# Expert stage with two 32-row half blocks per pass, each with its own expert's weights, from five weight buffers fed through one indirect queue

## The chip, the cores and the metric

The kernel runs on one core of one Trainium2 chip. The metric is the device time of one execution in microseconds (us); the median of three executions is given. A profile of one execution goes with it.

## The reference, cut to what matters

One step of a hybrid decoder for 512 prompt tokens and 64 sample tokens together (N = 576, D = 1024), all in 32-bit floats. After token mixing (convolution branch, sparse attention, output projection, layer norm) comes the channel stage, which the change is about:

```python
def hier_moe(x, w_rg, b_rg, w_re, b_re, w_eg, w_eu, w_ed):
    N = x.shape[0]
    gl = (x @ w_rg).astype(jnp.float32) + b_rg.astype(jnp.float32)
    pg = jax.nn.softmax(gl, axis=-1)
    grp = jnp.argmax(gl, axis=-1)
    ...
    top_p, top_i = lax.top_k(jax.nn.softmax(el_g, axis=-1), TOP_K_IN_GROUP)
    ...
    eid = grp[:, None] * EXPERTS_PER_GROUP + top_i
    ...
    hidden = jax.nn.silu(hg) * hu * combine[..., None].astype(x.dtype)
    return jnp.einsum('nef,efd->nd', hidden, w_ed)
x  = LN2(alpha * x1 + HierMoE(x1) + sigmoid(x1 @ w_pg) * (p[i] @ w_pp))
```

Every token goes to 2 of 32 experts, both of its one group of 8; so there are 1152 token-expert pairs. An expert's weights are a gate and an up matrix (1024 x 256 each) and a down matrix (256 x 1024): 3.146 MB. Run on its inputs, the reference's router gives experts 0 to 31 these numbers of pairs: 179 126 147 14 71 91 65 143 | 6 2 17 2 14 10 9 16 | 16 49 4 12 33 22 29 25 | 5 14 5 0 15 2 7 2.

## The kernel before, in words

All phases up to the layer norm LN1 (projection, convolution, index search, attention, w_o) stay as they are. The phases that matter here, in the order of TensorE's job list: the gate and embedding products `pg` and `pp` (L1145, L1152, L1393; weights on SyncE's queue through three buffers), among them `rank` (L1401: counts of pairs per expert and each pair's rank in its expert), and `slot_lists` (L1245: for each block the rows to gather); then the expert stage; then the sum of each token's two rows (L1573, L1581) with LN2.

Expert stage before. `blocks_and_slots` (L2293 on) turns the counts into blocks of 64 rows. Each of the 32 experts has one base block, whether it is full or not; 17 over blocks (NOVER) take what lies above 64 pairs of an expert. The 49 blocks run in a fixed order, base, base, over. A block is one pass: 64 rows of x1 are gathered into 128 partitions (row halves above each other, L1088, six buffers), transposed (L1507), multiplied with gate and up (L1525: 16 products, each a 128x64 stationary tile and 256 columns, gate in PSUM partitions 0 to 63, up in 64 to 127; every 32-bit product is two instructions), turned into `hid` by ScalarE and VectorE (L1889, L2363, L2367), transposed (L1535), multiplied with down (L1549: 4 products, 512 columns), copied to `ys` (L1895) and scattered (L1095).

Weights before. SyncE loads the base experts' weights with plain transfers into three buffers (L874 gate and up, L875 down); `up_in` and `down_in` are waited for apart. It issues the first three early (at 892 us of the span), and load e when the down product of base block e-3 is done (`y_full`). GpSimd loads the over blocks' weights with indirect transfers (L1073 into two buffers, L1080 into one); where a buffer already holds the expert, or the block is empty, the index is out of bounds and nothing moves, but the transfer is issued and signals its end.

TensorE works one pass ahead. The order of its instructions is written out, and it is the same before and after the change:

```python
            for p in range(NBLK):
                up_half(p, 0)
                if p:
                    hid_turn(p - 1)
                up_half(p, 1)
                if p + 1 < NBLK:
                    turn(p + 1)
                if p:
                    down(p - 1)
```

So `down(p)` comes after `up_half(p+1, 1)` and directly ahead of `up_half(p+2, 0)`. Each engine's instructions, GpSimd's transfers with their waits among them, run in program order.

## Time and profile before

| | |
|---|---|
| median of 3 executions | 1356.88 us (1349.61 to 1359.10) |
| profiled execution, span | 1355.7 us |
| TensorE matmul busy | 1207.4 us (89%) |
| VectorE / ScalarE / GpSimd busy | 765.2 / 411.4 / 573.1 us |
| first up product to last down product of the expert stage | 983.1 to 1315.8 us |
| moved by all transfers | 281.46 MB |

How to read it: the span of the profiled execution is 1.2 us under the median. Busy shares are averages over phases with different limits; the expert stage is a quarter of the span and has to be read by itself. SyncE and GpSimd issue transfers on two queues (q1 and q0 in the profile), which share the core's 16 DMA engines. PEclk 1.00 is TensorE at 2.4 GHz, 0.50 at 1.2 GHz.

### The profile page before, as it was taken

The numbers are of one execution on the slowest core, as the hardware profiler recorded it, in microseconds if no ns is written. First come the engines' busy times: TensorE is split into PE (matmuls) and PEld (weight loads), VectorE is DVE, ScalarE is ACT, GpSimd is POOL, SyncE is SP. The second block draws the span as 40 slices with busy tenths as digits, with TensorE's granted clock in tenths as the row PEclk, the third lists the DMA queues.
The fourth block names the chain that finished last, engine by engine and source line by source line (L and its number), as shares of the span: only waits on it lengthen the run. The fifth ranks groups of instructions, "written<-read, shape, count | busy, mean of one in ns | idle before, by whom it ended". The sixth has DMA issues, their size and how long they took to land.

```text
span 1355.7 us, 18796 instructions
## 1 busy us (share of the span) xinstructions
PE 1207.4 (89%) x7242; PEld 744.3 (55%) x7242; DVE 765.2 (56%) x1414; ACT 411.4 (30%) x852; POOL 573.1 (42%) x518
## 2 busy tenths in 40 slices
PE   4699999989499886878999899998998989998996
PEld 3425677777355543335565458887754544554542
DVE  1629999999987988696745134432622212222216
ACT  3450134364265467664121221231111111111110
POOL 5000067878776666657776000000233443443420
PEclk9799999989798987878999999999999999999998
DMA  9501222223266565658897630363199998999945
GB/s 326 192 27 36 93 63 63 63 82 116 72 199 179 156 198 169 203 178 249 298 300 235 208 98 31 95 271 132 43 394 421 389 416 345 368 416 419 400 156 205
DMA packets 92839, 281.46 MB, mean 208 GB/s; under 512 B 17959, under 2 KB 50551, under 8 KB 81799
## 3 DMA queue, kind: packets, MB, share of 16 engines
q1 hardware_dynamic: 54672, 165.64, 32.6%
q0 software_dynamic: 35520, 111.22, 24.7%
q10 hardware_dynamic: 2559, 3.40, 0.8%
q8 instruction: 58, 0.95, 0.3%
q14 instruction: 30, 0.25, 0.1%
HBM read 300.94 MB, written 23.11 MB: 239 GB/s over the span
## 4 chain that ended last, share of the span: by engine, by line
PE 49%; DVE 27%; DMA 10%; POOL 6%; issue 4%; ACT 3%; SPq 1%; POOLq 0%; DVEq 0%; ACTq 0%
PE ps L1525 10%; PE ps L1549 6%; POOL arena L1045 6%; DVE arena L1962 6%; DVE arena L1961 5%; DVE arena L1963 5%; PE ps L1139 5%; PE ps L1145 5%; PE ps L1369 4%; DMA arena<-scr_x,arena 3%; PE ps L1361 3%; DMA arena<-in_w_in 2%; DMA arena<-in_w_dn,arena 2%; PE ps L1507 2%; PE ps L1227 2%
## 5 line engine op out<-in xcount | busy, mean ns | idle before, releaser
L1045 POOL DMA_INDIRECT arena<-in_cache_kv,arena x256 | 267.7, 1046 | 125.2 <-issue 74.0
L1139 PE MATMUL ps<-arena 128*128 128x288 f32 (+2 forms) x1120 | 297.6, 427 | 1.1 <-ACT arena L1693 1.1
L1139 PEld LDWEIGHTS ps<-arena 128*128 128x128 f32 (+1 forms) x1120 | 211.0, 191 | 85.5 <-issue 30.0
L1525 PE MATMUL ps<-arena 128*64 128x256 f32 x1568 | 189.5, 384 | 5.6 <-DMA arena<-in_w_gu 3.5
L1525 PEld LDWEIGHTS ps<-arena 128*64 128x64 f32 x1568 | 109.2, 138 | 83.6 <-issue 28.0
L1095 POOL DMA_INDIRECT scr_ypair<-arena x49 | 50.5, 1030 | 184.5 <-ACT arena L1895 165.2
L1088 POOL DMA_INDIRECT arena<-scr_x,arena x49 | 50.0, 1021 | 172.1 <-DVE arena L2343 157.5
L1616 ACT ACTIVATE arena<-ps 128x256 f32<-128x256 f32 (+5 forms) x138 | 57.9, 429 | 203.9 <-PE ps L1361 64.4
L1024 POOL TENSOR_TENSOR arena<-arena 128x816 f32<-128x816 f32 x58 | 103.0, 1776 | 17.8 <-ACT arena L1634 11.2
L1145 PE MATMUL ps<-arena 128*128 128x256 f32 (+4 forms) x544 | 105.6, 357 | 0.9 <-ACT arena L1838 0.6
L1549 PE MATMUL ps<-arena 128*64 128x512 f32 x392 | 98.4, 624 | 8.0 <-DMA arena<-in_w_dn,arena 7.9
L1145 PEld LDWEIGHTS ps<-arena 128*128 128x128 f32 (+1 forms) x544 | 92.5, 194 | 14.0 <-issue 2.2
L2359 DVE COPY arena<-ps 128x512 f32<-128x512 f32 x49 | 33.9, 692 | 109.4 <-PE ps L1507 109.3
L2374 DVE COPY arena<-ps 128x128 f32<-128x128 f32 x49 | 14.3, 292 | 142.4 <-PE ps L1535 142.4
L1961 DVE MAX8 arena<-arena 128x8 f32<-128x2052 f32 x32 | 73.6, 2299 | 1.1
L1962 DVE FIND_INDEX8 arena<-arena 128x8 uint32<-128x2052 f32 x32 | 73.3, 2290 | 0.0
L1963 DVE MATCH_REPLACE8 arena<-arena 128x2052 f32<-128x2052 f32 x32 | 73.0, 2280 | 0.0
L1361 PE MATMUL ps<-arena 128*128 128x288 f32 (+1 forms) x192 | 68.1, 508 | 2.8 <-DVE arena L2148 2.2
L1895 ACT ACTIVATE arena<-ps 128x512 f32<-128x512 f32 x49 | 29.3, 597 | 122.5 <-PE ps L1549 122.5
L1634 ACT ACTIVATE arena<-arena 128x816 f32<-128x816 f32 x60 | 57.0, 970 | 28.6 <-POOL arena L1024 26.3
L1889 ACT ACTIVATE arena<-ps 128x128 f32<-128x128 f32 x49 | 13.6, 278 | 169.8 <-PE ps L1525 169.8
L2053 DVE SCALAR_TENSOR_TENSOR arena<-arena 128x512 f32<-128x512 f32 x120 | 56.9, 515 | 2.0
(350 smaller groups left out, 1687.1 us busy)
## 6 DMA issues: line engine op xcount, KB each, us to landing
arena<-in_w_gu SPq DMA_DIRECT2D x32, 2048.0 KB, 12.3
arena<-in_w_dn SPq DMA_DIRECT2D x32, 1024.0 KB, 15.6
arena<-in_w_in SPq DMA_DIRECT2D x20, 1024.0 KB, 5.6
arena<-scr_q SPq DMA_DIRECT2D x32, 256.0 KB, 4.6
arena<-in_cache_kv,arena POOLq DMA_INDIRECT x256, 3.9
arena<-in_w_o SPq DMA_DIRECT2D x4, 1024.0 KB, 5.4
arena<-in_w_pg SPq DMA_DIRECT2D x4, 1024.0 KB, 9.0
arena<-scr_ypair SPq DMA_DIRECT2D x4, 1024.0 KB, 8.0
```

The costliest lines, as they stand in the source:

```text
L1024: nc.gpsimd.tensor_tensor(a[:, 0:CLEN], a[:, 0:CLEN], p[:, 0:CLEN], ALU.add).then_inc(conv_add, 1)
L1045: pl.indirect_dma_start(unit_rows[:, 2 * j + t, half * H * HD:(half + 1) * H * HD], None, I["cache_kv"].rearrange("n (h d) -> (n h) d", h= ...
L1139: mm = nc.tensor.matmul(out, w[:, k], hT[:, k, a:b], start=(k == 0), stop=(k == KC - 1))
L1145: mm = nc.tensor.matmul(out, hT[:, k, at:at + rows], w[:, k], start=(k == 0), stop=(k == KC - 1))
L1361: mm = nc.tensor.matmul(ps[:, 0:n], w[:, c], src[:, c, at:at + n], start=(c == 0), stop=(c == CC - 1))
L1525: mm = nc.tensor.matmul(PS[2 + p % 2][64 * half:64 * half + 64, 0:2 * P], xT[:, p % 3, j, 64 * h:64 * h + 64], w[:, k, half, :], start=(k ...
L1549: mm = nc.tensor.matmul(PS[5 + p % 2][64 * half:64 * half + 64, :], hidT[:, p % 2, c * 64:c * 64 + 64], w[:, c, half * 512:(half + 1) * 51 ...
L1616: return nc.scalar.activation(handed(job, width, rows), PS[NUM[job] % RING][0:rows, 0:width], func, scale=scale)
L1634: nc.scalar.activation(prod[:, k % 3, 0:CLEN], glu[:, c, w:w + CLEN], cp, scale=tap).then_inc(prod_ready, 1)
L1961: step(V.max(m, work))
L1962: V.max_index(idxu[:, r * 8:r * 8 + 8], m, work)
L1963: step(V.match_replace(work, m, work, TAKEN))
```

## The change

Blocks have 32 rows (BLK) and no division into base and over: expert e has ceil(count/32) half blocks, and all half blocks are sorted by expert. A pass takes two half blocks, called visits 2p and 2p+1, each with its own expert's weights: `up_half` and `down` issue twice as many products, each with a 128x32 stationary tile, for four strips of 32 PSUM partitions (gate and up, times two visits). There are NBLK = 34 passes and NVISIT = 68 visits, which holds any routing.

Visit q uses weight buffer q % 5. `visit_blocks` cuts the sorted list into five runs (14, 14, 14, 13, 13 half blocks) and gives run j to buffer j, so neighbours in a run often share an expert. A visit whose buffer already holds its expert, or that is empty, gets an index out of bounds: its transfer is issued and moves nothing. Gate, up and down lie together in one array `w_ex` (24 KB a row); one indirect transfer of 3.146 MB, issued by GpSimd, fills a buffer and signals `expert_in[q % 5]`. SyncE loads no expert weights any more. The first three loads are issued once the table is ready, loads 3 and 4 after the last `pp` job, load q from 5 on when `y_full` says that pass (q-5)//2 has done its down product. `up_half(p, 0)` waits for the loads of visits 2p and 2p+1. The gather buffers are five, three of them filled first.

```diff
-BLK = 64
-NOVER = (2 * N - NE) // (BLK + 1)
-NBLK = NE + NOVER
-XR = 6
+BLK = 32
+NSLOT = 5
+NBLK = -(-(2 * N + NE * (BLK - 1)) // BLK // 2)
+NVISIT = 2 * NBLK
+XR = 5
+XEARLY = 3
 YR = 4
...
+def visit_blocks():
+
+    lengths = [len(range(j, NVISIT, NSLOT)) for j in range(NSLOT)]
+    return [sum(lengths[:q % NSLOT]) + q // NSLOT for q in range(NVISIT)]
+
+
+VISITS = visit_blocks()
...
-        ra = region(x_at, ki_at)
         rb = region(q_at + 2 * D, b_end)
         rk_ = region(ki_at + NT * D, q_at)
-        eset = [ra(3 * KC * F), rb(3 * KC * F), rb(3 * KC * F)]
+        ESIZE = 3 * KC * F
         w_at = x_at - WSLOTS * KC * GW
-        over_up = [view(ht_at + i * 2 * KC * F, (KC, 2, F)) for i in range(2)]
-        over_down = view(ht_at + 4 * KC * F, (FC, D))
-        assert ht_at + KC * N == w_at and 5 * KC * F <= KC * N + WSLOTS * KC * GW
+        assert ht_at + KC * N == w_at and ht_at + 2 * ESIZE >= x_at
+        eset = [rb(ESIZE), rb(ESIZE)] + [view(ht_at + i * ESIZE, (ESIZE,)) for i in (2, 0, 1)]
+        xg_at = ht_at + 3 * ESIZE
+        assert xg_at + XR * 512 <= ki_at
...
-                    for e in range(3):
-                        load_expert(e)
...
-            for e in range(3, NE):
-                sp.wait_ge(y_full, POS[("base", e - 3)] + 1)
-                load_expert(e)
...
+            def load_expert(q):
+                if q >= NSLOT:
+                    pl.wait_ge(y_full, (q - NSLOT) // 2 + 1)
+                pl.indirect_dma_start(eset[q % NSLOT], None, I["w_ex"],
+                                      bass.IndirectOffsetOnAxis(ap=widx[:, q:q + 1], axis=0),
+                                      bounds_check=NE * P - 1, oob_is_err=False).then_inc(expert_in[q % NSLOT], 16)
 
             def gather(p):
...
+            pl.wait_ge(wr_in, 48)
+            pl.wait_ge(full, after("pT", NT - 1))
+            nc.gpsimd.memset(xg[:, 0:XEARLY], 0.0).then_inc(xg_clear, 1)
+            pl.wait_ge(xg_clear, 1)
+            pl.wait_ge(table_ready, 1)
+            for q in range(3):
+                load_expert(q)
             pl.wait_ge(glist_ready, 1)
             pl.wait_ge(x1_out, 16 * NT)
-            for p in range(XR):
+            for p in range(XEARLY):
                 gather(p)
-            load_over_up(0)
-            load_over_down(0)
-            load_over_up(1)
+            pl.wait_ge(full, after("pp", 3, NT - 1))
+            for q in range(3, NSLOT):
+                load_expert(q)
+            pl.wait_ge(taken, TAKEN_AT[("pp", 3, NT - 1)])
+            nc.gpsimd.memset(xg[:, XEARLY:], 0.0).then_inc(xg_clear, 1)
+            pl.wait_ge(xg_clear, 2)
+            for p in range(XEARLY, XR):
+                gather(p)
             for p in range(NBLK):
                 if p and p + XR - 1 < NBLK:
                     gather(p + XR - 1)
+                for q in range(2 * p + NSLOT, 2 * p + NSLOT + 2):
+                    if q < NVISIT:
+                        load_expert(q)
                 scatter(p)
...
-                for half in range(2):
-                    for n in range(2 * NT):
-                        rows = TILES[n % NT][1]
-                        mm = nc.tensor.matmul(PS[4][64 * half:64 * half + 64, 0:NBLK], in_place[0:rows, n, :], in_block[0:rows, n, :],
-                                              start=(n == 0), stop=(n == 2 * NT - 1))
+                for n in range(2 * NT):
+                    rows = TILES[n % NT][1]
+                    for strip in range(4):
+                        mm = nc.tensor.matmul(PS[4][BLK * strip:BLK * strip + BLK, 0:NBLK], in_place[0:rows, n, :],
+                                              in_block[0:rows, n, strip % 2::2], start=(n == 0), stop=(n == 2 * NT - 1))
                 mm.then_inc(plist_full, 1)
...
             def up_half(p, part):
-                kind, n = BLOCKS[p]
-                k = n if kind == "base" else OVERS.index(n)
-                w = up_weights(eset[n % 3]) if kind == "base" else over_up[k % 2]
                 if part == 0:
-                    if kind == "base":
-                        pe.wait_ge(up_in[n % 3], 16 * (n // 3 + 1))
-                    else:
-                        pe.wait_ge(over_up_in[k % 2], 16 * (k // 2 + 1))
                     pe.wait_ge(xt_drained, p + 1)
                     if p >= 2:
                         pe.wait_ge(hid_ready, p - 1)
+                    for q in (2 * p, 2 * p + 1):
+                        pe.wait_ge(expert_in[q % NSLOT], 16 * (q // NSLOT + 1))
+                w = [up_weights(eset[q % NSLOT]) for q in (2 * p, 2 * p + 1)]
                 for k in range(4 * part, 4 * part + 4):
                     h, j = divmod(k, 4)
                     for half in range(2):
-                        mm = nc.tensor.matmul(PS[2 + p % 2][64 * half:64 * half + 64, 0:2 * P],
-                                              xT[:, p % 3, j, 64 * h:64 * h + 64], w[:, k, half, :],
-                                              start=(k == 0), stop=(k == KC - 1))
+                        for sub in range(2):
+                            r = 64 * half + BLK * sub
+                            mm = nc.tensor.matmul(PS[2 + p % 2][r:r + BLK, 0:2 * P],
+                                                  xT[:, p % 3, j, 64 * h + BLK * sub:64 * h + BLK * sub + BLK], w[sub][:, k, half, :],
+                                                  start=(k == 0), stop=(k == KC - 1))
...
             def down(p):
-                kind, n = BLOCKS[p]
-                w = down_weights(eset[n % 3]) if kind == "base" else over_down
-                if kind == "base":
-                    pe.wait_ge(down_in[n % 3], 16 * (n // 3 + 1))
-                else:
-                    pe.wait_ge(over_down_in, 16 * (OVERS.index(n) + 1))
+                w = [down_weights(eset[q % NSLOT]) for q in (2 * p, 2 * p + 1)]
                 pe.wait_ge(ht_drained, p + 1)
                 if p >= 2:
                     pe.wait_ge(y_act, p - 1)
                 for c in range(FC):
                     for half in range(2):
-                        mm = nc.tensor.matmul(PS[5 + p % 2][64 * half:64 * half + 64, :], hidT[:, p % 2, c * 64:c * 64 + 64],
-                                              w[:, c, half * 512:(half + 1) * 512], start=(c == 0), stop=(c == FC - 1))
+                        for sub in range(2):
+                            r = 64 * half + BLK * sub
+                            mm = nc.tensor.matmul(PS[5 + p % 2][r:r + BLK, :], hidT[:, p % 2, c * 64 + BLK * sub:c * 64 + BLK * sub + BLK],
+                                                  w[sub][:, c, half * 512:(half + 1) * 512], start=(c == 0), stop=(c == FC - 1))
                 mm.then_inc(y_full, 1)
...
-                nb, incl, base, t1 = [blocks[:, i, :] for i in range(4)]
-                step(V.tensor_scalar(nb, cnt, float(BLK), None, ALU.is_gt))
-                for k in range(2, -(-N // BLK)):
-                    step(V.tensor_scalar(t1, cnt, float(k * BLK), None, ALU.is_gt))
-                    step(V.tensor_tensor(nb, nb, t1, ALU.add))
+                nb, incl, base, whole = [blocks[:, i, :] for i in range(4)]
+                whole = whole.bitcast(I32)
+                step(V.tensor_scalar(whole, cnt, float(BLK - 1), None, ALU.add))
+                step(V.tensor_scalar(whole, whole, 5, None, ALU.logical_shift_right))
+                step(V.tensor_copy(nb, whole))
                 step(V.tensor_tensor_scan(incl, C["ones"][:, 0:NE], nb, 0.0, ALU.mult, ALU.add))
-                step(V.tensor_tensor(base, incl, nb, ALU.subtract))
-                V.tensor_tensor(cmp_, C["iota"][:, 0:NOVER].unsqueeze(2).to_broadcast([P, NOVER, NE]),
-                                incl.unsqueeze(1).to_broadcast([P, NOVER, NE]), ALU.is_ge)
-                step(V.scalar_tensor_tensor(base, base, float(BLK), C["overslot"], ALU.mult, ALU.add))
-                V.memset(turns[:, 0:2], -1.0)
-                step(V.tensor_reduce(table, cmp_, AX.X, ALU.add))
-                V.tensor_copy(turns[:, 2::2], table[:, 0:EARLY])
-                step(V.tensor_copy(turns[:, 3::2], table[:, EARLY:]))
-                now, last, other = turns[:, 2:], turns[:, 1:1 + NOVER], turns[:, 0:NOVER]
-                V.tensor_tensor(again[:, 0], now, other, ALU.is_equal)
-                V.tensor_tensor(again[:, 1], now, last, ALU.is_equal)
-                step(V.tensor_scalar(again[:, 2], last, float(NE), None, ALU.is_ge))
-                step(V.tensor_tensor(again[:, 2], again[:, 2], again[:, 0], ALU.mult))
-                step(V.tensor_tensor(again[:, 1], again[:, 1], again[:, 2], ALU.add))
-                for i in range(2):
-                    step(V.scalar_tensor_tensor(again[:, i], again[:, i], float(NE), now, ALU.mult, ALU.add))
-                V.tensor_scalar(widx, again[:, 0:2], float(P), C["part"], ALU.mult, ALU.add).then_inc(table_ready, 1)
+                V.memset(turns[:, 0:NSLOT], -1.0)
+                V.tensor_tensor(base, incl, nb, ALU.subtract)
+                step(V.tensor_tensor(cmp_, C["visit"].unsqueeze(2).to_broadcast([P, NVISIT, NE]),
+                                     incl.unsqueeze(1).to_broadcast([P, NVISIT, NE]), ALU.is_ge))
+                now, last = turns[:, NSLOT:], turns[:, 0:NVISIT]
+                step(V.tensor_reduce(now, cmp_, AX.X, ALU.add))
+                step(V.tensor_tensor(again, now, last, ALU.is_equal))
+                step(V.scalar_tensor_tensor(again, again, float(NE), now, ALU.mult, ALU.add))
+                V.tensor_scalar(widx, again, float(P), C["part"], ALU.mult, ALU.add).then_inc(table_ready, 1)
                 rk = ranks[:, 0:NT * NE].rearrange("p (t e) -> p t e", t=NT)
-                step(V.tensor_scalar(over, rk, float(BLK), None, ALU.is_ge))
-                V.tensor_tensor(rk, rk, C["baseslot"].unsqueeze(1).to_broadcast([P, NT, NE]), ALU.add)
-                step(V.tensor_tensor(over, over, base.unsqueeze(1).to_broadcast([P, NT, NE]), ALU.mult))
```

## Rows read from the trace of the kernel before

**Rows 1.** Windows: length, busy us by engine, PEclk, DMA share, GB/s.
```profile
983.00:1315.80 332.80, 315.26 (x2201) 160.92 (x2201) 73.61 (x205) 42.29 (x97) 126.50 (x125) 0.98 0.94 378
1000.00:1020.00 20.00, 20.00 (x143) 10.19 (x141) 4.80 (x14) 2.63 (x6) 8.18 (x8) 1.00 1.00 417
```
**Rows 2.** Timeline of TensorE, 1038 to 1062 us: start, length, what.
```profile
1040.90 1.95 PE L1525 MATMUL ps<-arena 128*64 128x256 f32 x16
1042.78 0.66 PE L1507 MATMUL ps<-arena 128*128 128x128 f32 x4
1047.39 3.68 PE L1549 MATMUL ps<-arena 128*64 128x512 f32 x8 [3.96 <-DMA arena<-in_w_dn,arena]
1050.86 2.67 PE L1525 MATMUL ps<-arena 128*64 128x256 f32 x16
...
1053.72 1.95 PE L1525 MATMUL ps<-arena 128*64 128x256 f32 x16
1055.60 0.66 PE L1507 MATMUL ps<-arena 128*128 128x128 f32 x4
1056.19 1.94 PE L1549 MATMUL ps<-arena 128*64 128x512 f32 x8
1057.95 1.90 PE L1525 MATMUL ps<-arena 128*64 128x256 f32 x16
...
1060.04 1.95 PE L1525 MATMUL ps<-arena 128*64 128x256 f32 x16
```
**Rows 3.** Groups by line and shape: engine, op, shapes, count, busy us, mean ns.
```profile
L1525 PE MATMUL ps<-arena 128*64 128x256 f32 x1568 | 189.5, 384 | 5.6 <-DMA arena<-in_w_gu 3.5 <-DVE arena L2359 1.9 <-DMA arena<-in_w_gu,arena 0.2
L1549 PE MATMUL ps<-arena 128*64 128x512 f32 x392 | 98.4, 624 | 8.0 <-DMA arena<-in_w_dn,arena 7.9
L1209 PE MATMUL ps<-arena 128*8 128x320 f32 x256 | 18.7, 432 | 0.0
```
**Rows 4.** Queues in the expert stage, 983.1 to 1315.8 us: packets, MB, share.
```profile
q1 hardware_dynamic: 8352, 91.23, 66.1%
q0 software_dynamic: 12176, 34.27, 27.0%
```
**Rows 5.** Timeline: ScalarE's copy, then GpSimd's transfers around 996 and 1297 us.
```profile
994.78 0.60 ACT L1895 ACTIVATE arena<-ps 128x512 f32<-128x512 f32 x1 [2.18 <-PE ps L1549]
996.21 1.03 POOL L1095 DMA_INDIRECT scr_ypair<-arena  x1 [10.55 <-ACT arena L1895]
...
1295.38 1.04 POOL L1080 DMA_INDIRECT arena<-in_w_dn,arena  x1 [0.30 <-issue]
1296.72 1.01 POOL L1073 DMA_INDIRECT arena<-in_w_gu,arena  x1 [0.30 <-issue]
```
**Rows 6.** Transfers issued at 1295.38, 1296.72, 1308.03, 1095.12 us: us to landing.
```profile
arena<-in_w_dn,arena POOLq DMA_INDIRECT x1, 2.1
arena<-in_w_gu,arena POOLq DMA_INDIRECT x1, 8.7
arena<-in_w_dn,arena POOLq DMA_INDIRECT x1, 5.8
arena<-scr_x,arena POOLq DMA_INDIRECT x1, 23.8
```
**Rows 7.** Chain of waits ahead of the expert stage: start, length, what.
```profile
913.57 8.72 DMA arena<-in_w_pp
...
922.33 6.41 PE ps L1393 x20
```
**Rows 8.** Timeline: SyncE's first expert load; the table's last steps; first gather.
```profile
892.36 0.58 SPq L874 DMA_DIRECT2D arena<-in_w_gu  x1
...
952.25 0.72 DVE L2299 TENSOR_TENSOR arena<-arena 128x544 f32<-128x544 f32 x1
...
955.39 0.24 DVE L2314 TENSOR_SCALAR arena<-arena 128x34 int32<-128x34 f32 x1
...
973.73 1.20 POOL L1088 DMA_INDIRECT arena<-scr_x,arena  x1 [157.52 <-DVE arena L2343]
...
983.06 3.67 PE L1525 MATMUL ps<-arena 128*64 128x256 f32 x32 [1.07 <-DVE arena L2359]
```

96 lines of the change are left out of this document (21 added, 75 removed).

## The prediction, made before the changed kernel was run

> **What bounds the kernel now.** I read the table of windows first, for the stretch that the change touches: between 983.0 and 1315.8 us TensorE is busy 315 of 332.8 us [rows 1]. So the expert stage is TensorE's, with the transfers close behind: in an undisturbed stretch they move 417 GB/s at a DMA share of 1.00, over the stage 378 GB/s [rows 1]. TensorE's timeline gives the pitch: the second half of the up product starts at 1053.72 and the next pass's at 1060.04, 6.32 us a pass [rows 2]. 49 passes are 310 us, and some 23 us are waits and what they leave behind. One such wait is in the same rows: TensorE stands 3.96 us, then the down product takes 3.68 us instead of 1.94 and the first half of the next up product 2.67 instead of 1.90. A wait of about 4 us costs another 2.5 us, because TensorE goes on at 1.2 GHz for some 5 us. Last the queues: q1 moves 91.2 MB (29 of the 32 base experts), q0 34.3 MB [rows 4].
>
> **How many loads the change makes.** This is counted from the routing. ceil(count/32) summed over the experts is 55 half blocks (30 of experts 0 to 7). The five runs take positions 0-13, 14-27, 28-41, 42-54 and 55-67 of the sorted list. So buffer 0 sees experts 0, 1, 2 (3 loads), buffer 1 sees 2 to 7 (6), buffer 2 sees 7 to 18 (12), buffer 3 sees 19 to 31 without 27 (12), and buffer 4 only empty visits. That is 33 loads, 104 MB, against 32 base experts and about 25 MB of over blocks before: counted in the same way, 8 gate/up loads and 9 down loads are 26.2 MB, and the row traffic of 1152 pairs is 9.4 MB, together 35.7 MB, where the row of q0 has 34.3 (a few gathers lie ahead of it) [rows 4]. The counting is sound.
>
> **Part 1, fewer passes.** 34 instead of 49. Is a pass as long as before? Up is 64 instructions instead of 32, each on a quarter of the array's columns. Today a 64-column instruction costs 189.5/1568 = 121 ns, 32 of them 3.87 us; down is 8 x 251 ns = 2.0 us. The nearest row with four strips is L1209: 18.7/256 = 73 ns for 320 columns, so 58 ns for 256 and 117 for 512: up 3.7 us, down 16 x 117 = 1.9 us [rows 3]. The strips overlap four deep, and I keep 6.32 us a pass. Bounds: 5.9 (an even better overlap, hardly any weight-load cost) and 6.9 (10% lost). By itself this takes 15 x 6.32 = 95 us off.
>
> **Part 2, when a load may start.** This decides. Load 2p+5 reuses the buffer of visit 2p and is issued when `down(p)` is done. TensorE's next instruction after `down(p)` is `up_half(p+2, 0)`, and that waits for visits 2p+4 and 2p+5. So the second visit of every pass gets its weights with no lead at all; the first visit's (2p+6, for pass p+3) have one pass. Before, load e had the over and base passes between base e-3 and e, three or four, for its lead. Now price it:
> - From `y_full` to GpSimd's transfer: ScalarE's copy ends at 995.38, the scatter waiting for it starts at 996.21, 0.83 us; two transfers in a row are 1.33 us apart [rows 5].
> - A transfer that moves nothing lands 2.1 us after its start on an idle queue, one of 1.05 MB after 5.8 us, one of 2.1 MB after 8.7 us [rows 6]. One step further, 3.15 MB after 11.6 us (with the 417 GB/s of [rows 1] from the 5.8 on: 10.8, the lower bound).
> - q0 is served in order: a gather of a few hundred KB issued behind weights took 23.8 us [rows 6]. So an empty transfer behind a full one is late too.
>
> So every pass from pass 2 on waits at least 0.83 + 2.1 = 2.9 us, even where nothing has to move; and where its second visit has a new expert, 0.83 + 11.6 = 12.4 us, plus 2.5 us at the low clock [rows 2].
>
> I went through the 34 passes with these numbers (transfers on q0 one after the other at 7.5 us for 3.146 MB, 1 us for a scatter and a gather between them):
> - 13 passes have a new expert in the second visit (5, 8, 11, 13, 16, 18, 20, 21, 23, 26, 28, 31, 33): 13 x 12.5 = 162.5 us, and 1.5 us where the queue was still at work. It is about every second visit of buffers 2 and 3.
> - 3 passes (3, 15, 25) have an empty second load behind a full first one: it lands 2.1 + 11.6 - 9.2 + 1 = 5.5 us late, 16.5 us.
> - 16 passes wait 2.9 us: 46.4 us. Pass 1 waits 3.3 us for load 3.
> - Low clock after the 16 long waits: 16 x 2.5 = 40 us.
>
> Together 270 us of waits. The other half of what the change brings, 23 MB less, is worth nothing: 33 x 7.5 = 248 us of transfers lie inside a stage of 486 us.
>
> The Trainium skill (DMA: Bandwidth & Descriptors, Anatomy of one DMA) fits a GpSimd transfer as 2.0 us + bytes/436 GB/s, 9.2 us for this load; by that the 13 long waits would be 31 us less and the time 1476. The rows are above it: 8.7 us for 2.1 MB, where the fit gives 6.8. The same page's Rules for kernel authors say to issue early and wait late; this change does the opposite for half its visits, and no other rule there weighs against that.
>
> **Part 3, ahead of the stage.** SyncE issues no expert loads at 892 us [rows 8]. These 9.4 MB lay ahead of the first `pp` slice, for which the chain waits 8.7 us from its issue, 913.57 to 922.28 [rows 7]; TensorE's share of that wait is about 4 us, and some low clock follows. I give 5 us back (bounds 0 and 6). All up to the end of `pp` moves 5 us earlier. Loads 0 to 2 are issued once the table is ready, today after L2314 at 955.6 [rows 8], then 950.6: some 3.5 us until bytes move (5.8 us less the 2.5 us that 1.05 MB take is 3.3 [rows 6]) and 3 x 7.5 us, so q0 is busy until 976.8. The first gather lies behind them and lands near 979 (today issued at 973.73). Transpose and copy follow, and the first up product starts at 980.5 instead of 983.06 [rows 8], a gain of 2.6 us. Bounds: 5 gained, 5 lost, if the gathers come later still. In the table, 14 small VectorE steps go, and compare and sum grow from 544 (0.72 us each [rows 8]) to 2176 elements, some 4 us more in place of 3 us: nothing. `slot_lists` has twice the instructions at half the width: nothing, `pp` follows it on TensorE. The tail stays.
>
> **The sum.** First up product 980.5; first pass 4.7 (no down product yet); 32 x 6.32 = 202.2; waits 162.5 + 1.5 + 16.5 + 46.4 + 3.3 = 230.2; low clock 15 x 2.5 = 37.5: pass 33 starts at 1455.3. Its up product at the low clock, down(32), the chain through `hid` and the last down product take 11.1 us: 1466.4. Today that point is 1315.8 [rows 1]. So +150.6 us on a span of 1355.7 us, 1506.3; the median is 1.2 us above the span, so **1507 us**. For this case alone: 10.8 us landing, 1.5 us of low clock and 5.9 us passes give 1455; 6.9 us passes and 3.5 us of low clock 1540.
>
> **The rivals.**
> - *The loads keep the queue full and TensorE only follows it* (faster). A stage of 33 x 7.5 us and 4 us at the ends, 252 us instead of 333, 5 us gained ahead: 1271 us. For it: today's DMA share is 1.00 in stretches of this stage [rows 1], and the bytes fall by a fifth. Against: only loads 2p+5 and 2p+6 can be outstanding, and buffers 0, 1 and 4, three of five, rarely bring one. It decides at the point where the 34 x 9.2 = 313 us that even empty transfers cost and some 10 us at the ends leave room: 338 us - 323 us, that is one long wait of 15 us. With two or more second visits that load, the change is slower. I count 13.
> - *The short waits let the clock drop as well.* A wait of 2.9 us lies under the one of 3.96 us that did it [rows 2]; if it is enough, 17 more passes pay 2.5 us, 42 us: 1549.
> - *The four strips don't overlap with 32-column tiles at this load.* Then up is 64 x 121 ns and down 16 x 251 ns, 5.9 us more a pass, not hidden by the waits, since the loads start after it: 1507 + 34 x 5.9 = 1707. Against: the 73 ns of L1209 [rows 3].
> - *The change doesn't do what it says:* if the sorted runs saved no load, all 55 visits would load and some 27 passes wait 15 us: 1650 and more. The routing counts speak against it.
>
> **How the numbers follow.** Forecast 0.74 (1455 to 1540), clock drop 0.13, faster 0.04, strips 0.03, no loads saved 0.02, and 0.04 for something that eats most of the loss but leaves it within 1% or a little slower. The range that leaves out no more than 2 in 10 is 1450 to 1555. About 1% is what a measurement of this kernel can tell from no change: faster 0.04, within 1% 0.03, slower 0.93.
>
> **What would show it.** In the changed profile: waits of `up_half` (L1525's successor) on `in_w_ex` of two sizes, 12 to 13 us 13 times and about 3 us 16 times, 230 us in all; a PEclk below 1.00 after each long one; up 3.7 to 3.9 us undisturbed; GpSimd's load issued 0.8 us after the down product's end; DMA moving about 104 MB of weights at a mean near 235 GB/s over the stage; the stage's first up product near 980 us and its last down product near 1466. It would be wrong if a full load landed in well under 10 us, if an empty transfer signalled without the 2 us, or if GpSimd issued load 2p+5 before `down(p)`.

## The result, and the profile after

The changed kernel takes 1518.61 us (median of 4 runs, 1514.29 to 1525.99), the kernel before 1355.74 us beside it (4 runs, 1349.61 to 1359.10). The ratio is 1.1207, interval 1.116 to 1.1254: slower, by 163 us. The profiled run of the changed kernel has a span of 1512.5 us, 6.1 us under its median.

The page of the changed kernel, groups by line (engine, op, shapes, count, then busy us, mean ns, then idle time ahead of them and what ended it):

```profile
L1483 PE MATMUL ps<-arena 128*32 128x256 f32 x2176 | 179.7, 487 | 222.4 <-DMA arena<-in_w_ex,arena 221.4
L1504 PE MATMUL ps<-arena 128*32 128x512 f32 x544 | 65.4, 598 | 0.4 <-DVE arena L2318 0.4
L1033 POOL DMA_INDIRECT arena<-in_w_ex,arena x68 | 67.9, 998 | 478.4 <-PE ps L1504 307.5
```

L1483 is the up product (before: L1525, [rows 3]), L1504 the down product, L1033 the load of a visit's weights. TensorE stands 221.4 us for weights in front of up products. The third row shows the other side of it: GpSimd stands 307.5 us ahead of these loads until a down product is done. The window of the stage, from the first up product to the end of the last down product (length, busy us by engine, PEclk, DMA share, GB/s), answers the first row of [rows 1]:

```profile
980.15:1472.80 492.65, 270.77 (x2886) 117.38 (x2886) 51.60 (x145) 29.12 (x67) 130.77 (x129) 0.78 0.54 210
```

The stage is 492.7 us instead of 332.8. TensorE works less (271 us instead of 315), and so do the 16 DMA engines (share 0.54 instead of 0.94): neither is the bound, they take turns. Queue q0 moves all of it now (queue, packets, MB, share; compare [rows 4]):

```profile
q0 software_dynamic: 14400, 103.05, 53.5%
```

The turns can be seen in the timelines of TensorE and of GpSimd, changed kernel, 1032 to 1069 us (start, length, what, idle time before it in brackets):

```profile
1032.52 1.92 PE L1504 MATMUL ps<-arena 128*32 128x512 f32 x16
1045.95 3.64 PE L1483 MATMUL ps<-arena 128*32 128x256 f32 x32 [11.50 <-DMA arena<-in_w_ex,arena]
1049.52 0.48 PE L1493 MATMUL ps<-arena 128*128 128x128 f32 x1
1049.92 1.94 PE L1483 MATMUL ps<-arena 128*32 128x256 f32 x32
1051.79 0.66 PE L1467 MATMUL ps<-arena 128*128 128x128 f32 x4
1052.38 1.92 PE L1504 MATMUL ps<-arena 128*32 128x512 f32 x16
1057.38 3.31 PE L1483 MATMUL ps<-arena 128*32 128x256 f32 x32 [3.08 <-DMA arena<-in_w_ex,arena]
...
1068.34 1.93 PE L1483 MATMUL ps<-arena 128*32 128x256 f32 x32 [3.08 <-DMA arena<-in_w_ex,arena]
```

```profile
1035.28 0.99 POOL L1033 DMA_INDIRECT arena<-in_w_ex,arena  x1 [6.07 <-PE ps L1504]
...
1055.15 1.00 POOL L1033 DMA_INDIRECT arena<-in_w_ex,arena  x1 [14.90 <-PE ps L1504]
```

A down product ends at 1034.4, GpSimd starts the load that waited for it at 1035.28, and TensorE's very next instruction can start only when it has landed, at 1045.95. The load at 1055.15 is an empty one and costs 3.08 us in the same place. The first half of the up product takes 3.64 us after the long wait, 3.31 after the short one behind it, and 1.93 us, full clock, after the next short one.

### The profile page after: what moved, and what is told of

It is laid out like the page before. It is cut to its first block, busy times and chain, and to the rows that moved or that the text cites. A ratio compares the mean times of both kernels' runs of the same rounds, so it can differ in the third digit from the quotient of the medians.

```text
span 1512.5 us, 19973 instructions
## 1 busy us (share of the span) xinstructions
PE 1155.9 (76%) x7967; PEld 696.2 (46%) x7967; DVE 741.5 (49%) x1331; ACT 398.1 (26%) x822; POOL 575.1 (38%) x523
## 4 chain that ended last, share of the span: by engine, by line
PE 45%; DVE 23%; DMA 18%; POOL 5%; issue 5%; ACT 3%; SPq 1%; POOLq 0%; DVEq 0%; ACTq 0%
DMA arena<-in_w_ex,arena 13%; PE ps L1483 11%; POOL arena L1013 5%; PE ps L1099 5%; DVE arena L1917 5%; DVE arena L1916 5%; DVE arena L1918 5%; PE ps L1504 4%; PE ps L1105 4%; PE ps L1329 4%; PE ps L1321 3%; DMA arena<-in_cache_kv,arena 2%; PE ps L1187 2%; PE ps L1467 1%; DMA arena<-in_w_pp 1%
## 5 line engine op out<-in xcount | busy, mean ns | idle before, releaser
L1483 PE MATMUL ps<-arena 128*32 128x256 f32 x2176 | 179.7, 487 | 222.4 <-DMA arena<-in_w_ex,arena 221.4
L1033 POOL DMA_INDIRECT arena<-in_w_ex,arena x68 | 67.9, 998 | 478.4 <-PE ps L1504 307.5
L1483 PEld LDWEIGHTS ps<-arena 128*32 128x32 f32 x2176 | 83.8, 136 | 312.6 <-issue 289.9
L2318 DVE COPY arena<-ps 128x128 f32<-128x128 f32 x34 | 9.9, 291 | 360.8 <-PE ps L1493 360.8
L1844 ACT ACTIVATE arena<-ps 128x128 f32<-128x128 f32 x34 | 9.4, 277 | 392.7 <-PE ps L1483 392.7
L992 POOL TENSOR_TENSOR arena<-arena 128x816 f32<-128x816 f32 x58 | 102.9, 1775 | 16.9 <-ACT arena L1589 10.2
L1504 PE MATMUL ps<-arena 128*32 128x512 f32 x544 | 65.4, 598 | 0.4 <-DVE arena L2318 0.4
L2303 DVE COPY arena<-ps 128x512 f32<-128x512 f32 x34 | 23.5, 691 | 75.2 <-PE ps L1467 75.1
L1329 PE MATMUL ps<-arena 128*128 128x256 f32 x256 | 55.9, 380 | 0.8 <-DVE arena L2072 0.8
L1139 PE MATMUL ps<-arena 128*128 128x128 f32 x256 | 40.1, 306 | 19.1 <-DMA arena<-in_cache_kv,arena 11.7
```

The costliest lines, as they stand in the source:

```text
L992: nc.gpsimd.tensor_tensor(a[:, 0:CLEN], a[:, 0:CLEN], p[:, 0:CLEN], ALU.add).then_inc(conv_add, 1)
L1033: pl.indirect_dma_start(eset[q % NSLOT], None, I["w_ex"], bass.IndirectOffsetOnAxis(ap=widx[:, q:q + 1], axis=0), bounds_check=NE * P - 1, ...
L1329: mm = nc.tensor.matmul(ps[0:rows, 0:GW], mixT[:, k, at:at + rows], w[:, k], start=(k == 0), stop=(k == KC - 1))
L1483: mm = nc.tensor.matmul(PS[2 + p % 2][r:r + BLK, 0:2 * P], xT[:, p % 3, j, 64 * h + BLK * sub:64 * h + BLK * sub + BLK], w[sub][:, k, half ...
L1504: mm = nc.tensor.matmul(PS[5 + p % 2][r:r + BLK, :], hidT[:, p % 2, c * 64 + BLK * sub:c * 64 + BLK * sub + BLK], w[sub][:, c, half * 512: ...
```

## The experiments

The chips of the first three groups of runs were slower than the one of the last group: the kernel before took 1480.66, 1481.90 and 1480.41 us there, 1351.46 in the last. For the changed kernel, which has a profile on either kind, the difference lies ahead of the expert stage: its first up product comes at 1115.5 us of the span there and at 980.2 on the chip of the result, and its stage is 487.2 us there and 492.7 here. What stands out in the profiles from the slower chips is idle time of TensorE that ends with nothing the profile shows (`<- issue`): 74 to 94 us of it ahead of the stage, in 78 to 92 places, in each of the eleven; none in the two profiles that the result compares, and none ahead of the stage in experiment 10, the last group. The largest group of it in the changed kernel's second profile:

```profile
PE ps L1162 <- issue: 35.4, 44, 4.3
```

L1162 is a product of the attention, far ahead of the expert stage. Experiment 4 comes back to this.

So what is compared is the ratio to the kernel before of the same group, and the length of the stage (first up product to last down product). The changed kernel once more, beside the second group:

> The changed kernel itself, unaltered, beside the others. The first four kernels ran on a chip on which the kernel before took 1481 us instead of 1356, so their times can't be set against the changed kernel's 1519 directly, only their expert stages can (492.7 us in the changed kernel, 332.8 in the one before). Theory: the expert stage is made of the same waits on any chip, 485 to 500 us; 155 to 165 us more than the kernel before, whatever the phases ahead take. Rival: the stage depends on the chip as the phases ahead do, then it is off by more than 10 us.

Measured: 1649.48 us, ratio 1.1165 (1.1104 to 1.1227), stage 487.2 us. TensorE's waits:

```profile
PE ps L1483 <- DMA arena<-in_w_ex,arena: 218.5, 33, 13.2
```

(us in total, times, longest). The loss is the same on both kinds of chip; 1649.48 and 487.2 are what the next runs are held against.

**1. The down product one half product earlier** (ScalarE's copies are swapped in the same way).

```diff
                     hid_turn(p - 1)
-                up_half(p, 1)
                 if p + 1 < NBLK:
                     turn(p + 1)
                 if p:
                     down(p - 1)
+                up_half(p, 1)
```

> The changed kernel with TensorE's order altered so that down(p-1) runs before the second half of up(p): hid_turn(p-1), turn(p+1), down(p-1), up_half(p,1). The same loads, bytes and instructions; only y_full comes 1.9 us earlier relative to the next up product. Theory (a load has no lead over its use): each of the 32 waits of pass 2 on loses 1.9 us, long ones 11.7 to 9.8, short ones 3.1 to 1.2, 62 us, and the half clock after the short ones goes, some 15 us: about 1440 against 1519. Rival (the weights move slower on GpSimd's one queue, or the queue is the bound): the bytes are the same, 1519 stays. Rival (products on 32 columns are slow): 1519 stays as well.

Measured: 1596.36 us, ratio 1.0794 (1.0727 to 1.0862), stage 443.6 us, 43.6 less than the changed kernel's. The waits of this kernel:

```profile
PE ps L1483 <- DMA arena<-in_w_ex,arena: 174.7, 33, 12.0
PE ps L1504 <- DVE arena L2318: 22.3, 17, 1.5
```

Nothing is loaded faster or less often here; each load only starts half an up product (1.9 us) earlier before its use. The short waits fall from 3.08 to 1.35 us, most long ones from 11.5 to between 9.7 and 10.3, and the sum falls by 44 us. A new wait takes 22 us back, that for the copy of `hidT`, which has less time now; as much comes from the clock, since behind a wait of 1.35 us the first half of the up product takes 1.93 us in every row, where it took 3.2 to 3.6 behind most waits of 3.08. So the lead of a load sets its wait, nearly one to one. The stage was expected to lose 77 us and loses 44; the new wait, which the expectation did not have, is the largest part of the difference.

**2. No empty transfers.** The 33 visits that load are written in for this routing, and the other 35 issue nothing and are not waited for.

```diff
+FULL = [0, 1, 2, 3, 6, 8, 11, 12, 17, 18, 22, 23, 26, 27, 28, 30, 32, 33, 37, 38, 41, 42, 43, 47, 48, 50, 52, 53, 56, 57, 58, 63, 67]
...
             def load_expert(q):
+                if q not in FULL:
+                    return
```

> The changed kernel without its 35 transfers that move nothing: the list of the 33 visits that really load is written into the program (counted from the routing of these inputs), the others issue nothing and nobody waits for them. Theory: the 16 waits of 3.1 us go and the half clock after most of them (1.3 to 1.5 us in about 12 passes); the 13 long ones stay at 11.7: 50 + 17 = about 67 us less, 1450. Rival (an empty transfer costs nothing by itself, TensorE would have waited for something else there, such as the gathered rows or the queue's real loads): 1519 to 1500.

Measured: 1590.80 us, ratio 1.0744 (1.0691 to 1.0798), stage 435.0 us. TensorE's waits:

```profile
PE ps L1488 <- DMA arena<-in_w_ex,arena: 180.7, 18, 15.4
```

The short waits are gone, 15 of 33, and the stage is 52 us shorter: 38 us of waits and the clock behind them. The long ones stay, 11.4 to 11.7 us apiece and up to 15.4 where two loads follow each other closely. The empty transfers are about a third of the loss (1.1165 to 1.0744).

**3. Four buffers instead of five.**

```diff
-NSLOT = 5
+NSLOT = 4
```

> The changed kernel with four weight buffers instead of five (runs of 17 half blocks, 32 loads instead of 33). Now both visits of pass p+2 reuse the buffers of pass p and are issued when down(p) is done, so no load has a lead. Theory: waits of 4.3 us where nothing moves (two transfers issued 1.33 us apart), 11.9 to 13.2 where one loads, about 19.4 where both do: some 360 us of waits instead of 218, about 1670. Rival (the total of bytes or the pace of the queue sets the stage): 32 loads instead of 33, 1510.

Measured (one run): 1805.67 us, stage 650.7 us:

```profile
PE ps L1483 <- DMA arena<-in_w_ex,arena: 362.3, 33, 19.2
```

With four buffers neither visit of a pass has a lead. The waits rise from 218.5 to 362.3 us in 33 places as before, and the kernel loses another 156 us.

**4. Gate/up and down loaded apart, each when its own product is done.** The up part of buffer q is released by the up product (`u_full`), nearly a pass earlier than by the down product; down weights are waited for ahead of `down`. In GpSimd's order each gather and each scatter moves behind the gate/up loads of one more pass.

```diff
+            def load_up(q):
+                if q >= NSLOT:
+                    pl.wait_ge(u_full, (q - NSLOT) // 2 + 1)
+                pl.indirect_dma_start(eset[q % NSLOT][:, 0:2 * KC * F], None, I["w_gu"],
...
+            def load_down(q):
                 if q >= NSLOT:
                     pl.wait_ge(y_full, (q - NSLOT) // 2 + 1)
+                pl.indirect_dma_start(eset[q % NSLOT][:, 2 * KC * F:], None, I["w_dn"],
```

> The changed kernel with each load in two transfers: gate and up (2.1 MB) into a buffer as soon as pass p has done its up product (u_full), down (1.05 MB) when it has done its down product (y_full); up waits for the first, down for the second. 136 instead of 68 weight transfers on the same GpSimd queue, the same 104 MB, the same products. Theory: gate and up now have a lead of 8 us and empty ones are never late; waits fall from 218 to some 50 us, but GpSimd issues six transfers of 1.33 us a pass, 8 us, more than TensorE's 6.3: a stage of 280 to 310 us, 1320 to 1350, below both kernels. Rival (GpSimd's queue is the bound of the changed kernel): twice the transfers, no faster than 1519. Rival (32-column products are slow): 1519 less nothing.

Measured: 1478.64 us, ratio 0.9996 (0.9969 to 1.0023), stage 328.5 us. In the second group:

> The kernel with gate/up loaded at u_full and down at y_full once more, beside the changed kernel. On the first chip its stage was 328.5 us, where 280 to 310 was forecast, with gaps of 0.4 to 0.8 us inside runs of products that no engine and no transfer released. Theory (those gaps belong to that chip): where they are absent the stage is 34 x 8.0 to 8.3 us, set by GpSimd's six transfers a pass, 275 to 300 us, and the time 3 to 5% below the kernel before. Rival (the gaps belong to this kernel): again about 328 us and equal to the kernel before.

Measured: 1480.75 us, ratio 0.9983 (0.9957 to 1.0009), stage 329.6 us. The waits of the first of the two in the stage:

```profile
PE ps L1497 <- issue: 27.9, 43, 0.8
PE ps L1497 <- DMA arena<-in_w_gu,arena: 7.8, 4, 2.8
```

All of the loss is gone with the lead given back: 218.5 us of waits for weights become 7.8. But the stage was expected at 280 to 310 us and is 328.5. Timeline of TensorE, `e4_split_again`, 1248 to 1257 us:

```profile
1248.63 1.48 PE L1497 MATMUL ps<-arena 128*32 128x256 f32 x18
1250.81 0.64 PE L1497 MATMUL ps<-arena 128*32 128x256 f32 x5 [0.69 <-issue]
1252.26 0.63 PE L1497 MATMUL ps<-arena 128*32 128x256 f32 x4 [0.82 <-issue]
1253.70 0.64 PE L1497 MATMUL ps<-arena 128*32 128x256 f32 x5 [0.80 <-issue]
1254.27 0.66 PE L1481 MATMUL ps<-arena 128*128 128x128 f32 x4
1254.86 1.92 PE L1520 MATMUL ps<-arena 128*32 128x512 f32 x16
1256.60 1.91 PE L1497 MATMUL ps<-arena 128*32 128x256 f32 x32
```

TensorE stands 0.7 to 0.8 us in the middle of a product, where the program has no wait: the half product that starts at 1248.63 takes 5.7 us, the one at 1256.60 takes 1.9. Over all products of the stage such idle time is 42.5 us in the first of the two profiles and 44.2 in the second. A stage of 328.5 us less 42.5 would be 286, inside what was expected; that is a subtraction and not a run. In the stage of the changed kernel there are no such rows, on either kind of chip: of the 222.4 us of idle time ahead of its up products 221.4 end with a load. But they are the same kind of idle time as the `<- issue` ahead of the stage, which only the profiles from the slower chips have, and both runs of this experiment were made on those. GpSimd's six transfers do not fill a pass either; it stands 2.5 us for an up product in each of these passes:

```profile
1245.07 1.00 POOL L1034 DMA_INDIRECT arena<-in_w_gu,arena  x1 [2.47 <-PE ps L1497]
...
1255.14 1.00 POOL L1034 DMA_INDIRECT arena<-in_w_gu,arena  x1 [2.49 <-PE ps L1497]
```

Experiments 7 and 8 ask what in this kernel brings the gaps out.

**5. The same, with load 2 behind the first gathers.**

```diff
-            for q in range(3):
+            for q in range(2):
                 load_up(q)
                 load_down(q)
...
                 gather(p)
+            for q in range(2, 3):
+                load_up(q)
+                load_down(q)
```

> As e4_split, but of the three loads that are issued once the table is ready only two go out then; the third is issued behind the first three gathers. Theory (expert weights ahead of it hold up the last 256 KB slice of the embedding product's weights, which took 17.9 us in the changed kernel and 2.9 without company): TensorE's wait for that slice falls from 7.9 us in e4_split to under 3, the first up product comes 5 to 8 us earlier, the time is 4 to 8 us less than e4_split. Rival (that slice waits for its own buffer): the wait stays at 8 us, the time is the same.

Measured: 1478.03 us, ratio 0.9973 (0.9946 to 0.9999); 2.7 us under `e4_split_again`, and the two intervals overlap: that the kernel is faster is not shown. In the profiles the wait for the last `pp` slice is 2.5 us instead of 7.7, and the first up product comes at 1103.8 instead of 1112.8; 9.0 us lie between the two in front, of which the wait is 5.2, and the stage is 3.3 us longer (332.8).

**6. Full loads by SyncE with plain transfers, no empty ones.** As experiment 2, the loads from visit 5 on by the other queue, with the experts written in.

```diff
+            for q, e in zip(FULL, EXPERT):
+                if q >= NSLOT:
+                    sp.wait_ge(y_full, (q - NSLOT) // 2 + 1)
+                    sp.dma_start(eset[q % NSLOT], I["w_ex"][e * P:(e + 1) * P, :]).then_inc(plain_in[q % NSLOT], 16)
```

> As e2_no_empty (33 loads, no empty transfers; the visits and experts written into the program from the routing of these inputs), but from visit 5 on the loads are plain transfers issued by SyncE, at the same points (y_full of the pass that last used the buffer). Theory (no lead, whichever queue): a long wait falls only by the 0.8 us of GpSimd's wake-up and the shorter start of a plain transfer, from 11.7 to 9.5 to 10.5 us; stage 435 - 13 x 1.7 = about 413 us. Rival (the single software queue makes the loads slow): waits of 6 us or less, stage below 370 us.

Measured (one run): 1576.05 us, stage 416.2 us:

```profile
PE ps L1497 <- DMA arena<-in_w_ex: 159.1, 17, 13.7
```

A wait is still 10.2 to 10.6 us in most places (11.4 to 11.7 with GpSimd's indirect transfers). The indirect queue costs about 1 us of a wait; the rest is 3.146 MB that start when they are needed.

**7. Half as many products, split loads.** Products with 64 columns as before the change. Gate takes the first visit's weights for all 64 rows and up the second's, so this kernel leaves out half of the mathematics; loads, waits and copies are those of 4.

```diff
-                        for sub in range(2):
-                            r = 64 * half + BLK * sub
-                            mm = nc.tensor.matmul(PS[2 + p % 2][r:r + BLK, 0:2 * P],
...
+                        mm = nc.tensor.matmul(PS[2 + p % 2][64 * half:64 * half + 64, 0:2 * P],
+                                              xT[:, p % 3, j, 64 * h:64 * h + 64], w[half][:, k, half, :],
...
```

> As e4_split (each load in two transfers, issued early), but with 64-column products instead of pairs of 32-column ones: 40 instead of 80 product instructions a pass. All loads, waits and copies stay, but every row is multiplied with only one of its pass's two sets of weights, so the mathematics of half the rows is left out. In e4_split TensorE stood 0.8 us again and again in the second half of the up product, four or five products at a time, with nothing that released it. Theory (TensorE's instructions come too slowly when it no longer waits for weights; their number doubled with the strips): the gaps go, a pass takes the 8.0 us of GpSimd's six transfers, stage 275 to 290 us instead of 329, time 40 to 50 us below e4_split. Rival (GpSimd or the transfers set e4_split's stage and the gaps fill idle time): 320 to 330 us as before.

Measured: 1458.68 us, ratio 0.9844 (0.9827 to 0.986), stage 310.9 us:

```profile
PE ps L1495 <- DMA arena<-in_w_gu,arena: 43.0, 15, 6.0
...
PE ps L1495 <- issue: 2.0, 3, 1.4
```

The gaps inside the up products go (2.0 us left; 12.8 over all products of the stage), and 35 us more wait for weights comes in their place. The time lies between the two expectations and settles neither.

**8. Split loads, no empty transfers, four strips as in the change.** The edits of 2 and 4 together.

> As e4_split, without the transfers that move nothing: 66 instead of 136 weight transfers on GpSimd (the visits that load are written into the program from the routing of these inputs), products with four strips as in the changed kernel. Theory (TensorE's instruction supply sets e4_split's 9.7 us a pass): GpSimd is relieved and nothing much is gained, stage 310 to 330 us. Rival (GpSimd's 8.0 us a pass set it): GpSimd needs 5.3 us a pass, the stage falls to the 250 to 280 us of the bytes.

Measured: 1444.51 us, ratio 0.9754 (0.9738 to 0.9771), stage 289.6 us:

```profile
PE ps L1504 <- DMA arena<-in_w_gu,arena: 37.5, 14, 7.4
...
PE ps L1504 <- issue: 1.9, 3, 0.8
```

All 64 instructions of each up product are there, and the gaps are nearly gone as well (L1504 is this kernel's up product; 10.0 us over all products of the stage, where `e4_split` has 42.5). The stage lies between the two expectations, nearer to the rival's. So the number of TensorE's instructions does not make them by itself; with half as many they go, and with the empty transfers away they go too. This kernel is 2.5% faster than the kernel before, but its visits are written in for this routing.

**9. The wide products of 7 in the changed kernel.**

> The changed kernel (loads as one transfer after down) with 64-column products instead of pairs of 32-column ones, 40 instead of 80 instructions a pass; again half the rows are not multiplied with their weights. Theory (the strips overlap four deep, and the waits for weights set the stage): 480 to 490 us as in the changed kernel's 487.2 on this kind of chip. Rival (32-column products, or their number, cost the changed kernel time): 20 us or more less.

Measured (one run): 1650.82 us, stage 487.1 us, against 1649.48 and 487.2.

```profile
PE ps L1481 <- DMA arena<-in_w_ex,arena: 216.5, 33, 12.9
```

In this kernel too each product with 64 columns takes one visit's weights for all rows. The four strips and the doubled instructions cost the changed kernel nothing.

**10. Only the second visits' loads split** (on the faster chip; load 2 behind the first gathers, as in 5).

```diff
+                if 2 * p + NSLOT < NVISIT:
+                    load_up(2 * p + NSLOT)
+                if NSLOT <= 2 * p + NSLOT - 2 < NVISIT:
+                    load_down(2 * p + NSLOT - 2)
+                if NSLOT <= 2 * p + NSLOT - 1 < NVISIT:
+                    load_whole(2 * p + NSLOT - 1)
```

> As e5_split_late, but only the second visit's load (2p+5) goes out in two transfers, gate/up at u_full and down at y_full; the first visit's (2p+6), which has a pass of lead anyway, is one transfer at y_full. GpSimd issues five transfers a pass instead of six, 6.7 us instead of 8.0; no routing is written into the program. Theory A (e8 showed it: GpSimd's transfers and the empty ones in the queue cost e4_split some 40 us): 34 fewer transfers give back 10 to 20 us, stage 310 to 320 us, 1460 to 1470, 1 to 1.5% below the kernel before. Theory B (lead is what counts): gate/up of the second visit now stand in q0 behind a whole 3.1 MB load issued a little earlier, waits of up to 8 us come back in a dozen passes, stage 335 to 355 us, 1485 to 1505.

Measured: 1390.27 us, ratio 1.0301 (1.0259 to 1.0343), stage 370.1 us:

```profile
PE ps L1504 <- DMA arena<-in_w_ex,arena: 118.6, 23, 11.4
...
PE ps L1374 <- DMA arena<-in_w_pp: 2.5, 1, 2.5
```

The loads that had no lead got one, and no wait of the stage ends with a split load any more. What waits now are the whole loads of the first visits (`in_w_ex`), 118.6 us. Their lead is a pass, some 6.5 us when nothing else waits, and a whole load needs about 11. In the changed kernel the waits of the second visits gave it the time; with those gone, as I read it, it shows. Against the changed kernel the stage is 122.6 us shorter. Both expectations were too low: the nearer one (lead is what counts) had 335 to 355 us for the stage. With five transfers a pass on this chip the stage has one stand without a releaser, 0.5 us.

## Why the prediction was right, point by point

The forecast was 1507 us, the median is 1518.6; by the profiled run, for which the sum was made, 1506.3 against 1512.5. The mechanism is the one named in part 2 of the prediction, and the runs show it: experiment 3 takes lead away and the waits grow, 1, 4 and 10 give lead and they fall, in 9 the strips change nothing. Of the 11.6 us between the medians, 6.2 are in the sum, 4.9 are that the median lies 6.1 us above the profiled span, not 1.2, and the rest is rounding. The upper bound for this case comes out of its three values; the lower one does not: 10.8 us landing, 1.5 us of low clock and 5.9 us passes give some 1465, not 1455. The measured time lies between the bounds either way.

The stage was to be 485.9 us (980.5 to 1466.4; the rounded terms give 485.7) and is 492.7. Term by term (a pass without its low clock is 6.49 us, as between the waits at 1068.34 and 1086.78; what a pass has above that is put down to the clock):

| term | forecast | measured |
|---|---|---|
| 13 long waits | 13 x 12.5 + 1.5 = 164.0 | 152.4 (11.50 to 11.95) |
| 16 short waits | 16 x 2.9 = 46.4 | 49.3 (3.07 to 3.11) |
| passes 3, 15, 25 | 16.5 | 12.8 (4.67, 4.28, 3.85) |
| pass 1 | 3.3 | 6.9 |
| low clock up to pass 32 | 37.5 | 49.1 |
| 32 passes | 32 x 6.32 = 202.2 | 32 x 6.49 = 207.7 |
| first and last pass | 15.8 | 14.4 |

- **Number and place of the waits:** as counted from the routing: the 13 long ones stand ahead of passes 5, 8, 11, 13, 16, 18, 20, 21, 23, 26, 28, 31 and 33, and q0 moved 103.05 MB in the stage: 30 loads of 3.146 MB (94.4), three being done before it, and some 9 MB of rows, as counted. Over the stage that is 210 GB/s where some 235 was named; the three loads ahead of it had been counted in.
- **The long wait** was sized 0.8 us too high. The landing was put at 11.6 us, one step beyond the 8.7 us of 2.1 MB [rows 6]; the lower bound named there, 10.8 us from the measured 417 GB/s [rows 1], is nearly the measured one: 11.72 - 0.83 = 10.9 us. The fit of the Trainium skill (DMA: Bandwidth & Descriptors, Anatomy of one DMA), 9.2 us by the prediction, is 1.7 us too low for this load.
- **The short wait** is 3.08 us where 0.83 + 2.1 = 2.9 was forecast.
- **Pass 1** waits 6.9 us instead of 3.3. Worked back from the prediction's own numbers, load 3 was to be issued at 976.9 (980.5 + 4.7 + 3.3 - 11.6). It was issued at 978.86, since the `pp` product that it follows came late (below), and landed 12.5 us later, at 991.33: 2.0 us and 0.9 us, and TensorE was ready 0.8 us earlier than forecast.
- **The clock** is the term where one of the rivals was partly right. A long wait costs 1.8 to 2.4 us at 1.2 GHz, 2.0 in the mean, not 2.5. But 13 of the 16 short waits cost 1.3 to 1.7 us as well, together 18.7 us; the prediction had given them nothing and put the other case at 42 us. In the stage this is the term that was put at nothing and wasn't. The three that are free are each the second of two short ones in a row (1068.34, 1109.30, 1413.16). With 23.8 us behind the 12 long waits up to pass 32 and 6.6 behind those of passes 1, 3, 15 and 25 the sum is 49 us where 37.5 stood: too much behind the long waits and nothing behind the short ones cancel in part, which is luck.
- **A pass** is 6.49 us instead of 6.32; undisturbed up and down products are as forecast (1.93 and 1.93, 1.92 us).
- **Ahead of the stage** the first up product came at 980.15, forecast 980.5, but by another way. TensorE starts the second `pp` stretch at 954.98, 16.5 us earlier than before (971.48). Some 5 us of this were there already at 865 us of the span, ahead of everything that the change touches, so they are a difference between two executions; the wait for the first `pp` slice is gone [rows 7], the products up to there ran at full clock, and those of `slot_lists`, which the prediction put at nothing, take 1.2 us instead of 3.3 (953.80 to 954.98, before 968.18 to 971.48). Then all but 3 us is given back, in a wait that the prediction did not have. Timeline of TensorE, changed kernel:

```profile
971.83 6.23 PE L1353 MATMUL ps<-arena 128*128 128x256 f32 x20 [12.12 <-DMA arena<-in_w_pp]
```

It is the last `pp` slice, 256 KB. Transfers of the changed kernel issued at 917.55 and at 953.91 us (count, KB, us to landing):

```profile
arena<-in_w_pp SPq DMA_DIRECT2D x1, 256.0 KB, 2.9
...
arena<-in_w_pp SPq DMA_DIRECT2D x1, 256.0 KB, 17.9
```

The second was issued behind loads 0 to 2 of the experts (944.3 to 946.9), 9.4 MB on the other queue. I had let these loads delay the gathers, which share their queue, and not the slice, which only shares the 16 engines. The gathers, which were to come near 979 us and set the first up product, had the first and third landed at 972.0 and 973.1. With two loads instead of three ahead of it the wait is 2.5 us (experiments 5 and 10). The step "all up to the end of `pp` moves 5 us earlier" was therefore wrong, and its result right by two errors that cancel.

- **The other rivals:** queue full and faster: no, the DMA share is 0.54. Strips that don't overlap: no (up 3.66 us; experiment 9). No loads saved: no (33 loads).

What stays open is the gaps of experiment 4: ahead of up products 28 and 32 us in 43 and 51 places, over all products 42.5 and 44.2 us. Among the kernels run on the slower chips the stage has them only with GpSimd's six transfers a pass and TensorE's 64 instructions an up product together, and hardly with either alone. Ahead of the stage every kernel run on those chips has such idle time, and no profile from the faster ones has more than 0.5 us. So that the gaps belong to those chips is a rival that nothing here excludes: the split kernel was not run on the faster kind, so what it takes there is open. Whether what is short is the supply of instructions, GpSimd, or the 16 engines, no run tells. Four longer stands ahead of down products remain in 7 and in 8 (10.4 and 6.8 us), as unexplained.

## What to carry to other kernels

When the order in which buffers are reused changes, ask for each load: what releases it, what needs it next, and how much work of the bounding engine lies between. Where that is nothing, the load's whole latency is on the path each time, however few bytes are left to move and however idle the queue is. A gain in passes and bytes (15 passes, 23 MB) is only worth something once that is paid; giving the load back nearly a pass of lead by freeing its larger part earlier was worth more here (11.8 points of the ratio) than any other single edit. Where a kernel has profiles from two chips, compare first the phases that no edit touches: idle time that they show on one chip alone cannot be put down to an edit without a run on the other.

## What the hardware showed that I had not expected

- A wait of 3.08 us can put the product behind it at 1.2 GHz or not. In the profile of the result it did where the pass before began with a wait of 4.67 us or more (13 times of 13) and did not where that pass began with another of 3.08 us (3 of 3). The second profile of the same kernel breaks both halves of that: there it did in 11 of 13 and in 2 of 4 places. So the wait of the pass before does not decide alone. Two rows of that profile; the pass before the first began with a wait of 12.26 us, the pass before the second with one of 3.06 us:

```profile
1501.93 1.93 PE L1483 MATMUL ps<-arena 128*32 128x256 f32 x32 [3.08 <-DMA arena<-in_w_ex,arena]
...
1542.25 3.34 PE L1483 MATMUL ps<-arena 128*32 128x256 f32 x32 [3.11 <-DMA arena<-in_w_ex,arena]
```

- Shorter waits can do it as well: behind one of 2.23 us in experiment 10 (1337.73 us) the half product takes 3.59 us. Behind waits of 1.35 us (experiment 1) it took 1.93 us each time, even right behind a pass with a long one.
- A small plain transfer (256 KB) beside 9.4 MB of loads on another queue took 17.9 us instead of 2.9. TensorE's wait for it was 10.6 us with whole loads and 7.7 with split ones in the same group of runs, and 2.5 with one load fewer ahead.
- Transfers that move nothing: without those of 35 visits (two each), the stage with split loads fell from 328.5 to 289.6 us, though TensorE hardly ever waited for one of them by name. Its idle time without a releaser fell from 42.5 to 10.0 us with them; as said, that may belong to the slower chips.
- The kernel before takes 1351 to 1356 us in two groups of runs and 1480 to 1482 us in three others on other chips. In the changed kernel, profiled on both kinds, the difference lies ahead of the expert stage, and 74 us of it are idle time of TensorE without a releaser, where the faster kind shows none.
